# Last gate tanh, gate stores and statistics' spreading placed behind a block's end; query regions cleared by GpSimd

## The reference

```
h = RMSNorm(x); z = h @ w_in
A: attention over compressed, selected and windowed keys, gated per head
B: dilated attention, three groups, merged by their softmax denominators
C: gated MLP inside chunks of 128
m = sum_i sigmoid(g_i) * (o_i @ w_branch_i);  x = x + m @ w_out
x = x + relu(RMSNorm(x) @ w_up)**2 @ w_down;  final RMSNorm
```

## Time and profile before

| | us |
|---|---|
| median of 3 runs | 1651.78 (1646.66 to 1652.04) |
| profiled execution, its own time | 1653.85 |
| its span, first to last instruction | 1651.0 |
| PE busy in the span | 1563.4 (95%) |
| DVE, ACT, POOL busy | 807.7, 308.5, 193.2 |

### The profile page before, as it was taken

One profiled execution on the slowest core, in us unless ns is written; L12 is line 12 of the kernel. 1 busy time (PEld: TensorE's weight loads), 2 busy tenths in 40 slices (PEclk: granted clock), 3 DMA queues, 4 the chain that ended last, 5 costly groups with the idle time before them and its releaser, 6 DMA issues. The chain is left out here.

```text
span 1651.0 us, 25883 instructions
## 1 busy us (share of the span) xinstructions
PE 1563.4 (95%) x9460; PEld 1249.2 (76%) x9460; DVE 807.7 (49%) x1757; ACT 308.5 (19%) x833; POOL 193.2 (12%) x333
## 2 busy tenths in 40 slices
PE   8998999999899999999887899899989999999996
PEld 4786878989778887877654466688868888888885
DVE  3442666675635546565633220044667666632234
ACT  2221244444401232222211321100010000000000
POOL 0001300000000000100275866200000000000000
PEclk9999999999989999999898899899999999999998
DMA  8998443444489999754599999764112222222221
GB/s 300 365 336 304 126 132 104 118 122 115 135 271 341 365 333 351 250 199 125 158 363 340 371 375 352 288 228 144 64 51 96 84 77 77 81 98 77 77 77 54
DMA packets 188975, 326.92 MB, mean 198 GB/s; under 512 B 21105, under 2 KB 123058, under 8 KB 187954
## 3 DMA queue, kind: packets, MB, share of 16 engines
q1 hardware_dynamic: 157138, 182.78, 33.9%
q0 software_dynamic: 27104, 129.65, 21.8%
q10 hardware_dynamic: 4608, 12.85, 2.1%
HBM read 307.73 MB, written 109.32 MB: 253 GB/s over the span
## 5 line engine op out<-in xcount | busy, mean ns | idle before, releaser
L1659 PE MATMUL bank<-hT,big 128*128 128x272 f32 x704 | 182.3, 400 | 1.9 <-PEq L1339 1.2
L1659 PEld LDWEIGHTS bank<-hT,big 128*128 128x128 f32 x704 | 130.1, 192 | 30.4 <-issue 4.2
L2670 PEld LDWEIGHTS bank<-hT,xk 128*128 128x128 f32 x512 | 97.7, 196 | 48.3 <-issue 25.8
L2670 PE MATMUL bank<-hT,xk 128*128 128x272 f32 x512 | 130.3, 409 | 1.4 <-ACT gst L2680 1.1
L2925 PE MATMUL bank<-hT,wring 128*128 128x272 f32 x392 | 95.4, 392 | 0.0
L1070 PEld LDWEIGHTS bank<-big,w 128*128 128x128 f32 x768 | 88.5, 192 | 7.9 <-issue 7.5
L1070 PE MATMUL bank<-big,w 128*128 128x128 f32 x768 | 93.4, 278 | 0.0
L1659 PE MATMUL bank<-ht,big 128*128 128x272 f32 x352 | 91.0, 393 | 0.0
L2925 PEld LDWEIGHTS bank<-hT,wring 128*128 128x128 f32 x392 | 74.5, 190 | 15.3
L2925 PE MATMUL bank<-aT,wring 128*128 128x272 f32 x352 | 85.9, 392 | 0.0
L2268 POOL DMA_DIRECT2D ring<-in_sel_pages x144 | 81.0, 563 | 41.0 <-issue 16.0
(11 more groups left out here) (476 smaller groups left out, 2680.9 us busy)
## 6 DMA issues: line engine op xcount, KB each, us to landing
out_new_dil<-in_cache_dil POOLq DMA_DIRECT2D x8, 8176.0 KB, 47.2
wring<-in_w SPq DMA_DIRECT2D x84, 512.0 KB, 3.7
big<-in_w SPq DMA_DIRECT2D x63, 512.0 KB, 9.4
big<-in_cmp_pages SPq DMA_DIRECT2D x128, 128.0 KB, 2.3
out_new_dil<-in_cache_dil POOLq DMA_DIRECT2D x8, 2032.0 KB, 14.9
ring<-in_sel_pages SPq DMA_DIRECT2D x144, 64.0 KB, 6.4
ring<-in_sel_pages POOLq DMA_DIRECT2D x144, 64.0 KB, 5.4
big<-in_cmp_pages SPq DMA_DIRECT2D x128, 64.0 KB, 1.9
```

What stands on the lines that cost most here:

```text
L1659: mm = pe.matmul(product_bank(p, n), w[:, P * k:P * k + P], HH[x][:, k, :], start=(k == 0), stop=(k == 3))
L2670: mm = pe.matmul(gate_bank(h), gw[u % 2][:, P * k:P * k + P], hT[:, k, HT * hf:HT * hf + HT], start=(k == 0), stop=(k == KD - 1))
```

## The change

The tanh of the last two gates (6 and 7), their two stores and the spread of statistics 3 are moved from the dilated block to the head of ACT's list in the sample block: first `last_gates_act` (two tanh, then for each a wait for it and the issue of its store), then the two gate loads and `cmp_exp_act` as before, then `spread_stat(act, 3)`. SP's waits at the end of the dilated block ask for two gate stores fewer. In their place SP waits for these two stores in the sample block, ahead of quad 4.

The clearing of the two halves of `lq` moves from DVE in the sample block to POOL in the dilated block, behind a wait for the last step's values on PE and the third join on DVE, and for the second half one for the stores of new rows. The clearing of `imp` on DVE moves behind the first half's copies.

```diff
--- before.py
+++ after.py
@@ -1561,6 +1561,7 @@
             return t, i, wc, max(0, i - 1), wc // P + 2
 
         FLIPS = 2
+        LQ = 4 * 3 * 136
 
 
 
@@ -1686,13 +1687,30 @@
                     if p:
                         act.wait_ge(s_ps, 7 * (p - 1) + 2)
                     act.activation(px, product_bank(p, 1), ACT.Copy).then_inc(s_px, 1)
-                if n == 3:
+                if n == 3 and p < DPAIRS - 1:
                     for u in range(2):
                         s = 2 * p + u
                         if is_gate(s):
                             act.wait_ge(s_ps, 7 * p + 7)
                             act.activation(unit_home(s), unit_home(s), ACT.Tanh, scale=0.5
                                            ).then_inc(s_gt, 1)
+
+        def last_gates_act(act):
+            for g in (GP - 2, GP - 1):
+                home = unit_home(36 + g)
+                act.activation(home, home, ACT.Tanh, scale=0.5).then_inc(s_gt, 1)
+            for g in (GP - 2, GP - 1):
+                act.wait_ge(s_gt, g + 1)
+                act.dma_start(t["scr_gates"][g], unit_home(36 + g)).then_inc(s_gs[g % 2], 16)
+
+        def spread_stat(eng, p):
+            eng.wait_ge(s_so, STORED + 16 * (p + 1))
+            if p:
+                eng.wait_ge(s_cb, p)
+            for hh in range(2):
+                eng.dma_start(spread[hh * DH:hh * DH + DH, :, :, :].rearrange("p o k q -> p (o k q)"),
+                              t["scr_stat"][p, hh:hh + 1, :].to_broadcast([DH, 2048])
+                              ).then_inc(s_bc, 16)
 
         def turned(s):
 
@@ -1969,15 +1987,6 @@
                     sp.dma_start(t["scr_stat"][p].rearrange("h (r n) -> (h r) n", n=P), stat_row
                                  ).then_inc(s_so, 16)
 
-                def spread_stat(p):
-                    sp.wait_ge(s_so, STORED + 16 * (p + 1))
-                    if p:
-                        sp.wait_ge(s_cb, p)
-                    for hh in range(2):
-                        sp.dma_start(spread[hh * DH:hh * DH + DH, :, :, :].rearrange("p o k q -> p (o k q)"),
-                                     t["scr_stat"][p, hh:hh + 1, :].to_broadcast([DH, 2048])
-                                     ).then_inc(s_bc, 16)
-
                 sp.dma_start(con[:, C_MD:C_WD], t["con"][:, C_MD:C_WD]).then_inc(s_m4, 16)
                 for p in range(3, DPAIRS):
                     if p == 18:
@@ -1991,11 +2000,11 @@
                         store_turn((p - 8) // 5)
                     if p % 5 == 2 and p > 7:
                         store_stat((p - 12) // 5)
-                        spread_stat((p - 12) // 5)
+                        spread_stat(sp, (p - 12) // 5)
                     if p % 5 == 4 and p > 4:
                         store_new((p - 9) // 5)
                 store_stat(2)
-                spread_stat(2)
+                spread_stat(sp, 2)
                 store_turn(3)
                 store_new(3)
                 load_early(sp, 0)
@@ -2003,18 +2012,20 @@
                 for g in range(4, 6):
                     store_gate(g)
                 load_early(sp, 1)
-                for g in range(6, GP):
-                    store_gate(g)
-                spread_stat(3)
                 for i in range(2):
                     sp.wait_ge(s_st[i], 32)
-                    sp.wait_ge(s_gs[i], 16 + 16 * GP // 2)
+                    sp.wait_ge(s_gs[i], 16 * GP // 2)
                 sp.wait_ge(s_nd, 96 * 4)
                 sp.wait_ge(s_row, 16)
 
             @block.gpsimd
             def _(pool):
                 bulk_copies(pool, len(bulk) - sent["n"])
+                pool.wait_ge(s_fl, GROUPS2 + group_at(STEPS - 1, "sum") + 1)
+                pool.wait_ge(s_cb, 3)
+                pool.memset(w1f[:, 0:LQ], 0.0)
+                pool.wait_ge(s_nd, 96 * 4)
+                pool.memset(w1f[:, LQ:2 * LQ], 0.0)
 
             @block.scalar
             def _(act):
@@ -2163,7 +2174,6 @@
         dd = sb("dd", [P, 2], p4)
         om = con[:, C_HEAD + GB * 512:C_HEAD + GB * 512 + P]
 
-        LQ = GB * 3 * 136
         lq = [w1f[:, LQ * i:LQ * i + LQ].rearrange("p (j g c) -> p j g c", j=GB, g=3)
               for i in range(2)]
         omD = w1f[:, 2 * LQ:2 * LQ + 512]
@@ -2698,6 +2708,9 @@
                                      .rearrange("b s n -> s b n")).then_inc(s_dn, 16)
 
                 for n in range(2, NQ):
+                    if n == 4:
+                        for i in range(2):
+                            sp.wait_ge(s_gs[i], 16 + 16 * GP // 2)
                     load_quad(sp, mybir.EngineType.SP, 0, n)
                 for k in range(2):
                     sp.dma_start(vnew[32 + S * k:32 + S * k + S, :, :], t["scr_v"][:, k, :].rearrange(
@@ -2716,9 +2729,11 @@
 
             @block.scalar
             def _(act):
+                last_gates_act(act)
                 gate_load(act, 0)
                 gate_load(act, 1)
                 cmp_exp_act(act)
+                spread_stat(act, 3)
                 for gg in range(2):
                     for c in range(9):
                         mid, end = gate_halves(gg, c, True)
@@ -2754,9 +2769,7 @@
             @block.vector
             def _(dve):
                 ch = dve_chain.on(dve)
-                ch.count(dve.memset(imp[:, :], 0.0))
                 for gg in range(2):
-                    ch.link(dve.memset(lq[gg][:, :, :, :], 0.0))
                     for g in range(3):
                         for hh in range(2):
                             rows = slice(hh * DH, hh * DH + DH)
@@ -2767,6 +2780,7 @@
                                     "p k (j s) -> p j k s", j=GB))
                     last.then_inc(s_lq, 1)
                     if gg == 0:
+                        ch.count(dve.memset(imp[:, :], 0.0))
                         cmp_max_dve(dve, ch)
                 window_dve(dve, ch, 0)
                 cmp_probs_dve(dve, ch)
```

## The result

The changed kernel takes 1656.08 us (median of 20 runs, 1651.52 to 1661.37) against 1651.69 for the kernel before (20 runs beside it): ratio 1.0026, 95% interval 1.0016 to 1.0035. It is 4.4 us slower; the forecast was 2.0 us faster. The change is inside the 0.5% that the prediction called "same", but the sign is the other one, and with this many runs it can be told. The time lies 1.1 us above the end of the range given.

The account below looks back on a forecast made before the run. The sample block was taken as bound by its transfers: of the barrier's -3.4 us, -2.0 reaches the end, from the median 1651.78 to 1649.8. Forecast 1648.4 to 1651.3 (chance 0.51); wider range 1643.5 to 1655.

Parts of the forecast that it names:

- The barrier: Ahead of the sample block: DVE's last sum arrives last, PE starts at 809.1 instead of 812.5, -3.4 us (bounds -1.8 and -3.4).
- The first gate product: On PE behind the barrier: starts near 818.6 after waiting for its weights, against 821.67 before, a gain of 3.1 us.
- The spread's price: Spread moved behind cmp_exp_act, to about 813.5, 3.4 us later: costs nothing, since its reader, the join, starts at 838.54.
- The transfers: Sample block's pages: start 3.4 us earlier, lead 0.1 to 0.5 MB by 820; -2.0 us taken, carried to the end.
- bytes alone decide: Rival, chance 0.15: nothing of the front's gain reaches the end, time 1651 to 1652 us.
- The waits at 843 and 875: PE's waits for selected keys: the one at 843 starts some 3 us earlier and is longer, keys start near 841.
- last sign: The prediction falls if waits for quads in the rest of the block come out by more than 3 us otherwise.
- SP held ahead of quad 4: Rival, chance 0.12: SP waits there for both last stores, delaying later quads; 1655 us at 10 us landing, 1660 at 15.
- POOL holds the barrier: Rival, chance 0.10: at 3.73 us a clear, 1.6 of the 3.4 us are gone; time 1650.5 to 1651.8.
- the front's whole gain reaches the end: Rival, chance 0.12: waits at 843 and 875 come from page issue, not bytes; gain 5 to 9 us, 1643 to 1647.
- The clock: PE's granted clock behind the barrier: stands at 1.00, where it was 0.50 from 812.5 to 820 before.

Follow-up runs that it names:

- clears alone: Kernel before, with only the two clears of lq moved from DVE to POOL: 1653.42 us, ratio 1.0003.
- stores alone: Changed kernel with the spread issued by SP ahead of the barrier and the clears on DVE in the sample block again: 1650.38 us, ratio 0.9983.
- clears behind the copies: Changed kernel with the spread on SP ahead of the barrier, POOL's clears also waiting for DVE's copies of the compressed queries: 1646.74 us, ratio 0.9971.
- two queues ahead of the barrier: As clears behind the copies, with the spread's second half issued by ACT ahead of the barrier, the first by SP: 1648.14 us, ratio 0.9978.
- weights first, wait at quad 4 and at 5: As clears behind the copies, ACT loading gate weights before its gate stores; SP's wait for them ahead of quad 4: 1651.48 us; quad 5: 1647.80.
- spread alone: Kernel before, with only the spread moved behind the barrier, on ACT behind the compressed exp: 1659.53 us, ratio 1.0039.
- later: Changed kernel with the spread on ACT moved behind the gate of the block's first step, issued at 831.38: 1656.86 us, ratio 1.0031.
- another source: Changed kernel with the spread replaced by two same-size loads to 64 partitions, reading 64 different cache rows instead of one repeated: 1655.52 us, ratio 1.0025.
- two queues: Changed kernel with the spread's second half issued by SP behind its pages of quad 2, the first half by ACT: 1657.26 us, ratio 1.0027.
- short rows: As another source, but four loads of 64 partitions by 4 KB in place of two by 8 KB: 1655.27 us, ratio 1.0022.

## Why the prediction was wrong, step by step

**The barrier: right.** "-3.4 us" was forecast, and 3.20 came. PE's idle time there fell from 4.63 to 0.80, and DVE was the last to arrive, as written: its last sum ends at 809.51 + 0.44 = 809.95, and the scores start at 810.27. Three terms inside were off. A clear on POOL took 1.46, near the lower bound of 1.42, not 2.5; that changed nothing, since POOL was done before DVE either way:

```profile
803.57 1.46 POOL L2026 MEMSET w<- 128x1632 f32 x1 [93.25 <-DVE obT L1960]
804.97 1.46 POOL L2028 MEMSET w<- 128x1632 f32 x1
```

(The factor of 1.96 that the prediction quoted from the Trainium skill, GPSIMD Engine Reference, section 3.1, is one for an add. For this clear the two engines' rows stand at 1.46 and 1.42; the line-rate of its section 4.1 comes nearer.) And beside the clears DVE's copies were held, which the prediction did not see. DVE's last sum ended 0.63 later than forecast (808.37 + 0.95 = 809.32), and PE followed it by 0.32 instead of 0.7, which took back half of that; this much is luck. In DVE's timeline after:

```profile
803.75 3.03 DVE L2105 COPY big<-qaS 64x128 f32<-64x128 f32 x2
...
809.51 0.44 DVE L1723 TENSOR_TENSOR dq<-bank,con 128x272 f32<-128x272 f32 x1 [0.36 <-PE bank L1660]
```

**The first gate product: right.** Forecast near 818.6 after a wait for its weights; with this execution's offset of 0.95 that is 819.55, and it was 819.53. So near a hit is partly luck: ACT issued 0.28 earlier than forecast, and the load took 7.6 instead of 7.3. The wait for `lq` shrank from 1.76 to 0.39, under the half microsecond given.

**The spread's price: the step that failed.** The prediction wrote of the spread "Its reader, the join, starts at 838.54, so this costs nothing", and under "The transfers" it let "the same 1.6 MB" run "on ACT's queue amid the pages" at "325 to 385 GB/s". Both are false for the spread. Its reader does wait for nothing, but the pages that share the engines with it do. In the stretch that holds it the core moves 204 GB/s. The lead of 0.1 to 0.5 MB by 820, by which the sum was bounded, is a lag: from 808 the kernel before had moved 2.9 MB by 820 and 4.7 by 825, the changed one, each time 0.95 us later, 2.7 and 3.8.

How much of the engines the spread takes can be read from the rows of one DMA queue, 808 to 835 (packets, MB, share of the 16 engines). Its bytes are those of ACT's stores and weights, with the spread where ACT issues it: the changed kernel first, then the spread back on SP, then the 128 partitions.

```profile
q10 hardware_dynamic: 736, 2.65, 33.8%
```
```profile
q10 hardware_dynamic: 579, 1.62, 17.4%
```
```profile
q10 hardware_dynamic: 864, 2.65, 29.0%
```

The spread's share is 33.8 - 17.4 = 16.4% of 27 us, 4.4 us, and on 128 partitions 3.1. To these come the pages beside it, which are slowed as well. The block lost 5.00 where the forecast had it lose 1.4. That 4.4 and 5.00 lie so close shows the order of size and no more, since the waits later in the block swing by several us. With this one term taken out, that is with the spread back on SP, the kernel gains 3.0 us (1648.85 against 1651.82 beside it), inside the forecast's 0.5 to 3.4.

The kernels sort themselves by the spread's place and form. The block, in us, each from one profiled execution:

| the spread or its substitute | block |
|---|---|
| issued ahead of the barrier | 256.26 (before), 256.23 (clears alone), 257.15 (stores alone), 255.38 (spread back on SP), 252.10 (clears behind the copies), 255.24 (two queues ahead of the barrier), 257.91 and 253.91 (weights first, wait at quad 4 and at 5) |
| in the block, on 128 partitions | 257.38 |
| in the block, on 64 partitions | 261.26 (after), 260.58 (spread alone), 263.96 (later), 260.98 (another source), 261.70 (two queues), 260.19 (short rows) |

The first group and the last don't overlap.

**What the profile before already showed.** The spread was slow in its old place too. It was issued at 810.07, and its two transfers took

```profile
DMA to landing us min/median/max: 5.2/6.1/7.1
```

to land, so it ran into the sample block's first 3 to 5 us. That is the stretch of 233 GB/s at a share of 1.05 in the earlier trace rows. The prediction used this 233, and took the rise from 233 to 385 as a sign against its rival that bytes alone decide, without asking what ran there. It could have priced the spread from that row. The old place was cheaper all the same: the spread began ahead of the pages, while the DMA engines had nothing but the last stores (share 0.04 from 808 to 810). With the spread back on SP it is issued at 803.97, and SP's pages begin at 810.76. Moving only the tanh and the stores gains 0.2% (0.9983, and 0.9978 with the clears moved too, both intervals just below 1).

**The waits at 843 and 875: wrong.** The selected keys that started at 843.03 were to start near 841 after a longer wait. They start at 847.27 and wait for nothing, because PE, held at quad 2, comes too late for any wait there:

```profile
847.27 1.04 PE L2401 MATMUL bank<-ring,big 128*32 128x512 f32 x8
```

The wait of 7.74 at 875.63 is gone too. By the prediction's own last sign, waits that come out otherwise by more than 3 us, it falls here.

**The second stretch.** From 840 to 850 the core moves 280 GB/s after, and moved 349 before. POOL's issues stand still for 8.77 us ahead of 843.12 there, behind PE's late products on quad 2 (832.79, at a granted clock of 0.66 from 830 to 840). That this is a consequence of the first wait is argued from the order of events; no run tested it alone.

**Rivals.** *SP held ahead of quad 4* did not decide: the stores landed 2.8 to 5.5 us after issue, and SP went on at 817.57. But the mechanism is real. With the stores behind the weights SP is held to 822.38, and the ratio goes from 0.9971 to 0.9993 (the intervals overlap a little); with the wait one quad later it is 0.9969. *POOL holds the barrier* and *the front's whole gain reaches the end* are refuted by the rows above. *Bytes alone decide* is refuted for this spread: the same bytes on 128 partitions left a block of 257.38, and on 64 one of 260.98 (the intervals of the two ratios, [0.9971, 1.0015] and [1.0009, 1.0040], still overlap a little). On 128 partitions the rival fits: 1651.83 lies in its 1651 to 1652, and the gain of the barrier is used up.

**The clock.** The granted clock stood at 1.00 from 810 to 815, as forecast. Behind PE's wait of 4.88 us it was 0.68 from 815 to 820 and 0.64 from 820 to 825, and the gate products of the block took 136.5 us in all after against 130.3 before. How much of that reached the end is open, since PE waits for pages in between.

## What to carry to other kernels

Before moving a transfer off a barrier, ask what it runs beside in its new place, and not only whether its reader is late: a transfer with no waiting reader still takes its share of a stream that something waits for. Price it by its shape too, not by its bytes alone: beside a transfer that reaches only 64 partitions the core moved little more than half its rate here, pages included. A stretch in which the DMA engines have nothing else is the place for such a transfer. A low rate at a full share in the profile before is the sign to look for. Moving only what gates the barrier, here the tanh and the stores, kept the gain.

## What the runs showed of the hardware

*A transfer to 64 partitions in a full stream.* 204, 224 and 211 GB/s over 820 to 825 with 64 partitions (spread, another source, short rows), 385 with 128, 374 without any; the share of busy engines was 1.00 to 1.06 in all five. The Trainium skill, SBUF — State Buffer, "Door 1: The DMA port swizzle (why `[64,N]` ≈ `[32,N]`)", says that partitions 0 to 63 lie behind 8 of 16 ports, and gives 196 GB/s for 64 partitions and 328 for 128 at 1 MiB. The rates here lie near these, but they are of all that the core moves, not of the transfer alone; the ports themselves no run here shows. By the page's 196 GB/s the spread is an estimated 5.4 us of the stream, and the queue's rows above give 4.4. Other queues' pages are slowed along with it: SP's pages of quad 2 took 12.2 us to land, 8.8 beside the 128 partitions, and 6.9 with the spread ahead of the barrier.

*Copies on DVE beside a clear on POOL.* The two copies of 64 x 128 took 2.75 and 0.27 us with the clears on POOL at the same time, and 0.54 together when POOL waited for them. The Trainium skill, SBUF — State Buffer, "Who interferes with whom", says that a VectorE copy in a two-port mode and a GpSimd instruction lock each other out for the whole instruction. That these copies ran in such a mode no row shows, but the rows agree: the first clear starts at 803.57, ahead of the first copy at 803.75; that copy ends at 803.75 + 2.75 = 806.50, just behind the end of the second clear at 804.97 + 1.46 = 806.43; and the copies are short again when the clears wait for them.
